# Attention of a hybrid encoder: value products straight behind the scores, transposes over three banks

## The chip, the cores and the metric

The kernel runs on one core of a Trainium2 chip. A core has TensorE (PE in the profile; PEld is its loading of weights), VectorE (DVE), ScalarE (ACT), GpSimd (POOL) and SyncE, whose queue (SPq) issues the transfers here. All data are float32. The metric is the time of one execution on the device in microseconds.

## The reference

Two layers act on two sequences, of 512 and 2048 tokens, 1024 wide. Each layer makes one input projection, then three branches (a recurrence in both directions, attention, a gating branch), and one output projection. The change touches attention alone:

```python
s = einsum('bqhd,bkhd->bhqk', q, k) * 96 ** -0.5     # 6 heads, q and k 96 wide (64 + 32 rotary)
p = softmax(s, axis=-1)
o = einsum('bhqk,bkhd->bqhd', p, v)                  # v 64 wide
```

Each sequence attends to itself, all keys for every query.

## The kernel before, in words

`build` runs the stages of a layer one after the other; each ends with a barrier of all engines. `mla_attention` (L1582) is the fourth of five stages. It reads queries and keys, already transposed (`qkt`, 96 rows per head), and values (`va`) from memory in HBM, and writes `ob`.

Work goes in **slots**, 17 for each of 6 heads, 102 in all (`slots`). Slot 0 of a head is the whole short sequence: four tiles of 128 queries against 512 keys. Each other slot is one tile of 128 queries of the long sequence against its 2048 keys. Either way the scores are 128 x 2048 numbers in banks 0 to 3 of the eight PSUM banks (512 columns of float32 each). Four slots of the long sequence (`TPG`) make a **group**, and so does a head's slot 0: five groups a head.

What happens to slot n:

- `scores(n)` on TensorE: products of 64 rows (two at a time side by side in the array, L1746) and of 32 rows (four side by side, L1751), added in the bank. A bank may be written when the exponentials of slot n-1 have read it (`freed`).
- `maxima(n)` on VectorE: maximum of each row, in two halves (L1875), times -scale (L1877). For a head's slot 0 it is one step over four banks (L1869).
- `exponentials(n, half)` on ScalarE: exp of 1024 columns (L1830), or four of 512 in a head's slot 0 (L1827), into `pr[:, n % 2]`. `exp_count` says how many must be done for each part.
- `turn(n, x)` on TensorE for the parts x = 0 to 3 of 512 columns: four transposes of 128 x 128 into one bank (L1770), 4 for even parts and 5 for odd ones. It waits until the part before in the same bank has been copied.
- `turned_out(n, x)`: the copy of that bank to `PT` in SBUF, parts 0 and 2 by ScalarE (L1839), parts 1 and 3 by VectorE (L1884). ScalarE copies part 0 before its exponentials of the next slot and part 2 behind them.
- `weigh(g, i)` on TensorE: the value products of group g, a pair of key blocks at a time, each of 64 output rows, two side by side (L1786), into bank 6. The list `due` gives each iteration up to two pairs of a group whose last slot lies at least two iterations back. There are 107 iterations; 0, 1, 3, 4 and 5 have no pair, all others have two. From slot 102 on there are only value products.
- When a group is complete (`summed_in`), ScalarE copies bank 6 to `oT` (L1857), TensorE turns it back in iteration n+1 (`turn_out`, four transposes, L1796, into bank 7), and VectorE divides by the sums (`normalise`, L1889 to L1900).

TensorE's order in iteration n is written out: scores of n; part 0 of slot n-1; `turn_out`; part 1; the value products; parts 2 and 3. VectorE's is maxima of n, copy of part 1, `normalise`, copy of part 3.

Each engine executes its own instructions in order; waits are on semaphores that another engine counts up. `act_t` and `dve_t` count the copies, `scored`, `exps`, `turned`, `summed`, `o_out`, `o_turned` and `normed` the other steps.

Transfers are all issued by SyncE in order. At the start of the stage come two for slot 0 of head 0 (`first`), then six for the queries of its other slots (columns 512 to 2560; 64 rows twice, 32 rows four times, as each tile of the array needs its own copy), six for the keys, one for the values, and then head 1. Slot 1 of head 0 waits for the twelve (`arrived[0]`).

Of the kernel before, what the change touches and what calls it, by code (L numbers as in the profile page):

```python
# [27 lines left out]
P = 128  # L28
# [3 lines left out]
T = T0 + T1  # L32
# [1549 lines left out]
def mla_attention(l, late, late_in, nc, d, ps, kc, col, amod, eps, ident):  # L1582
# [6 lines left out]
    KB1 = T1 // P  # L1589
    slots = [(h, s) for h in range(HB) for s in range(NSLOT)]  # L1590
    NS = len(slots)
    BANK_T, BANK_O, BANK_F = 4, 6, 7
    HALF = (slice(0, DN), slice(DN, P))
    STRIP = [slice(DR * n, DR * (n + 1)) for n in range(4)]
    KEYS = (0, 2, 1, 3)
# [23 lines left out]

    def summed_in(n):  # L1620
        return [g for g, i in due[n] if final_pair((g, i))] if 0 <= n < len(due) else []

    def buffer_user_before(g):

# [6 lines left out]
    with ExitStack() as ctx:  # L1631
# [28 lines left out]

        bank = lambda b: ps[:, b, :].rearrange("p (j c) -> p j c", c=P)

        with stage(nc, "in0 in1 first_in v_in0 v_in1 scored maxed exps turned act_t dve_t summed o_out o_turned normed sent0 sent1 zeroed chain") as (
                block, in0, in1, first_in, v_in0, v_in1, scored, maxed, exps, turned, act_t, dve_t, summed, o_out, o_turned, normed, sent0, sent1, zeroed, chain):
            arrived, v_in, sent = (in0, in1), (v_in0, v_in1), (sent0, sent1)

            @block.sync
            def _(sp):
# [31 lines left out]

                for n in range(2):
                    sp.dma_start(first[:, n, :], d["qkt"][HB * DQK * n:HB * DQK * n + DQK, 0:T0]).then_inc(first_in, 16)
                load_queries(0, T0, T, arrived[0])
                load_keys(0, arrived[0])
                load_v(0)
                load_head(1, arrived[1])
                load_v(1)
# [19 lines left out]
            def _(pe):  # L1727
                def scores(n):
                    h, s = slots[n]
                    w = heads_in[h % 2]  # L1730
                    if h == 0 and s == 0:
                        pe.wait_ge(first_in, 32)
                        for c in range(4):
                            pe.matmul(ps[:, c, :], first[:, 0, c * P:(c + 1) * P], first[:, 1, :], start=True, stop=True).then_inc(scored, 1)
                        return
                    if s == (1 if h == 0 else 0):
                        pe.wait_ge(arrived[h % 2], 16 * 18 * (h // 2 + 1) - (16 * 6 if h % 2 == 0 else 0))

                    def freed(c):
                        if n:  # L1740
                            pe.wait_ge(exps, exp_count[n - 1][c])

                    def rows64(c):
                        t, k0 = (c, 0) if s == 0 else (TPG - 1 + s, T0 + G * (KEYS[c] % 2))
                        q, k = w[HALF[c % 2], Q_N + t * P:Q_N + (t + 1) * P], w[HALF[c % 2], K_N + k0:K_N + k0 + G]
                        return pe.matmul(ps[:, c, :], q, k, start=(c < 2), stop=(c >= 2))  # L1746

                    def rows32(c):
                        t, k0 = (c, 0) if s == 0 else (TPG - 1 + s, T0)
                        r = STRIP[KEYS[c]]  # L1750
                        return pe.matmul(ps[:, c, :], w[r, Q_R + t * P:Q_R + (t + 1) * P], w[r, K_R + k0:K_R + k0 + G], start=(c >= 2), stop=(c < 2))  # L1751

                    for c in range(2):
                        freed(c)
                        rows64(c)
                    for c in range(4):
                        if c >= 2:
                            freed(c)
                        last = rows32(c)
                        if c < 2:  # L1760
                            last.then_inc(scored, 1)
                    for c in range(2, 4):
                        rows64(c).then_inc(scored, 1)

                def turn(n, x):
                    pe.wait_ge(exps, exp_count[n][x])
                    if 2 * n + x // 2:
                        pe.wait_ge(dve_t if x % 2 else act_t, 2 * n + x // 2)
                    for k in range(TPG):
                        last = pe.transpose(ps[:, BANK_T + x % 2, k * P:(k + 1) * P],  # L1770
                                            pr[:, n % 2, (TPG * x + k) * P:(TPG * x + k + 1) * P], ident)
                    last.then_inc(turned, 1)

# [16 lines left out]

                def turn_out(g):
                    pe.wait_ge(o_out, g + 1)
                    if g:
                        pe.wait_ge(normed, g)
                    for j in range(TPG):
                        last = pe.transpose(ps[:, BANK_F, j * P:(j + 1) * P], oT[:, g % 2, j * P:(j + 1) * P], ident)  # L1796
                    last.then_inc(o_turned, 1)

                for n in range(len(due) + 1):
                    now = due[n] if n < len(due) else []  # L1800
                    if n < NS:
                        scores(n)
                    turns = 1 <= n <= NS
                    if turns:
                        turn(n - 1, 0)
                    for g in summed_in(n - 1):
                        turn_out(g)
                    if turns:
                        turn(n - 1, 1)
                    for u in now:  # L1810
                        weigh(*u)
                    if turns:
                        turn(n - 1, 2)
                        turn(n - 1, 3)

            @block.scalar
            def _(a):
# [16 lines left out]
                def turned_out(n, x):  # L1834
# [1 line left out]
                    if before is not None:  # L1836
                        a.wait_ge(summed, before + 1)
                    a.wait_ge(turned, 4 * n + x + 1)
                    a.activation(evict_target(n, x), bank(BANK_T), ACT.Copy).then_inc(act_t, 1)  # L1839

                for n in range(len(due)):
                    turns = 1 <= n <= NS
                    if n == 0:
                        a.wait_ge(zeroed, 2)
                    if turns:
                        turned_out(n - 1, 0)
                    if n < NS:
                        exponentials(n, 0)
                    if n < NS:
                        exponentials(n, 1)  # L1850
                    if turns:
                        turned_out(n - 1, 2)
                    for g in summed_in(n):
                        a.wait_ge(summed, g + 1)
                        if g >= 2:
# [4 lines left out]
            def _(v):  # L1860
# [18 lines left out]
                def turned_out(n, x):  # L1879
# [1 line left out]
                    if before is not None:  # L1881
                        v.wait_ge(summed, before + 1)
                    v.wait_ge(turned, 4 * n + x + 1)
                    v.tensor_copy(evict_target(n, x), bank(BANK_T + 1)).then_inc(dve_t, 1)  # L1884

                def normalise(g):
                    h, k = divmod(g, GROUPS)
# [2 lines left out]
                    ch.wait()  # L1890
                    ch.link(v.reciprocal(rec[:, 1, :], rec[:, 0, :]))
                    v.wait_ge(o_turned, g + 1)
                    b = ps[:, BANK_F, :].rearrange("p (j c) -> p j c", c=P)
                    ch.link(v.tensor_copy(halves[:, :, :], b[:, :, 0:DV]))
                    ch.wait()
                    ch.link(v.tensor_tensor(halves[:, :, :], b[:, :, DV:P], halves[:, :, :], ALU.add))
# [4 lines left out]
                                    rec[:, 1, :].unsqueeze(2).to_broadcast([P, TPG, DV]), ALU.mult).then_inc(normed, 1)  # L1901

                for n in range(len(due) + 1):
                    turns = 1 <= n <= NS
                    if n < NS:
                        maxima(n)
                    if turns:
                        turned_out(n - 1, 1)
                    for g in summed_in(n - 1):
                        normalise(g)  # L1910
                    if turns:
                        turned_out(n - 1, 3)


def out_projection(l, late, late_in, cols, sg, nc, d, ps, kc, col, amod, eps, ident):
# [359 lines left out]
```

## Time and profile before

| | us |
|---|---|
| timed, median of 3 runs | 5414.87 (5413.25 to 5425.9) |
| the profiled execution | 5432.9 |
| its span, first to last instruction | 5430.8 |
| TensorE busy in the span | 5145.1 (95%) |
| VectorE busy | 2809.7 (52%) |
| ScalarE busy | 2067.7 (38%) |
| transposes of the attention stages, L1770 | 456.4 |
| value products, L1786 | 370.7 |
| scores, L1746 and L1751 | 231.7 + 230.2 + 117.9 + 117.1 |

Of this span slots 1 to 101 of the first layer take 1622.95 to 2353.96 us, and those of the second begin at 4344.02.

How to read the rows below. A line of the timeline has the start, the length, the engine, the line of the kernel, the operation, what it writes and reads, how many instructions stand in it one behind the other, and in brackets how long the engine had been idle before and who ended that. A matmul's printed length includes its way through the array, so neighbouring lines overlap by about 0.1 us: the distance from one start to the next is what a block really costs. Instructions side by side in the array are counted singly (one float32 product of the scores stands as two instructions). The second view gives for each stretch its length, the busy time of each engine with its number of instructions, the granted clock of TensorE as a share of 2.4 GHz, the busy share of the DMA engines and GB/s.

### The profile page before, as it was taken

The page shows a single profiled execution, that of the slowest core. Times are in us where ns is not written, and L with a number is a line of the kernel's source. Part 1 is how long each engine was busy: PE and PEld are TensorE (multiplying, and loading weights), DVE is VectorE, ACT ScalarE, POOL GpSimd, SP SyncE. Part 2 cuts the span into 40 slices and gives each one's busy share as a digit, 9 for nine tenths or more (in the row PEclk, how much of TensorE's full clock was granted, in tenths as well). Part 3 has the DMA queues.
Part 4 walks back from the last instruction along what each step waited for, and adds up shares of the span by engine and source line. Part 5 has one row for each costly group of instructions (what it writes and reads, how often), then busy time and mean ns, then how long its engine had stood idle before and what let it go on. Part 6 is the DMA issues. An engine that isn't in the chain of part 4 may idle for free. (4 is left out here: it accounts for less than half of the span.)

```text
span 5430.8 us, 98183 instructions
## 1 busy us (share of the span) xinstructions
PE 5145.1 (95%) x40460; PEld 2723.0 (50%) x40460; DVE 2809.7 (52%) x4438; ACT 2067.7 (38%) x3470; POOL 642.5 (12%) x1110
## 2 busy tenths in 40 slices
PE   8999999999979999989989999998899799999899
PEld 3444344478864444434434444444778644444454
DVE  2222387655545565556522214875555455555565
ACT  1121456345545454421112115562455444454211
POOL 0000000044430000001100000000444300000011
PEclk9999999999989999989999999999999899999999
DMA  5311565466551222135343115655555411221353
GB/s 225 141 68 57 185 216 195 156 164 164 146 126 30 46 60 52 37 134 214 111 163 141 68 56 195 217 198 155 151 156 148 117 39 40 57 60 37 108 177 116
DMA packets 579384, 668.56 MB, mean 123 GB/s; under 512 B 231216, under 2 KB 458032, under 8 KB 568384
## 3 DMA queue, kind: packets, MB, share of 16 engines
q1 hardware_dynamic: 578352, 661.17, 39.6%
q8 instruction: 326, 5.34, 0.4%
q14 instruction: 114, 0.93, 0.1%
q10 hardware_dynamic: 592, 1.11, 0.1%
HBM read 395.02 MB, written 267.13 MB: 122 GB/s over the span
## 5 line engine op out<-in xcount | busy, mean ns | idle before, releaser
L490 PE MATMUL ps<-feat_hT,w_features 128*128 128x512 f32 x2240 | 974.2, 593 | 0.0
L810 PE MATMUL ps<-w_tokens,prep_hT 128*128 128x512 f32 (+1 forms) x1920 | 821.7, 588 | 22.0 <-DMA prep_hT<-s_ht 22.0
L490 PEld LDWEIGHTS ps<-feat_hT,w_features 128*128 128x128 f32 x2240 | 421.0, 190 | 507.1 <-issue 504.0
L1875 DVE TENSOR_REDUCE att_mx<-ps 128x1 f32<-128x1024 f32 x384 | 453.5, 1220 | 287.7 <-PE ps L1751 285.3
L810 PEld LDWEIGHTS ps<-w_tokens,prep_hT 128*128 128x128 f32 x1920 | 363.5, 191 | 468.8 <-issue 441.4
L2156 PE MATMUL ps<-w_out,fin_yT 128*128 128x512 f32 x1280 | 569.0, 598 | 2.5 <-DVE fin_yT L2106 2.5
L1770 PEld LDWEIGHTS ps<-kc,att_pr 128*128 128x128 f32 x3264 | 350.8, 140 | 323.4 <-issue 275.6
L1839 ACT ACTIVATE att_PT<-ps 128x512 f32<-128x512 f32 x384 | 229.2, 597 | 631.2 <-PE ps L1770 628.0
L1770 PE MATMUL ps<-kc,att_pr 128*128 128x128 f32 x3264 | 456.4, 280 | 6.0 <-ACT att_PT L1839 2.7
L1830 ACT ACTIVATE att_pr<-ps,att_nb 128x1024 f32<-128x1024 f32 x384 | 424.8, 1111 | 68.7 <-DVE att_nb L1877 68.7
L1884 DVE COPY att_PT<-ps 128x512 f32<-128x512 f32 x384 | 264.1, 688 | 284.5 <-PE ps L1770 283.7
L2156 PEld LDWEIGHTS ps<-w_out,fin_yT 128*128 128x128 f32 x1280 | 238.9, 192 | 274.9 <-issue 271.6
L1786 PE MATMUL ps<-att_PT,att_V 128*64 128x512 f32 x1536 | 370.7, 604 | 0.0
L380 ACT ACTIVATE feat_z<-ps 128x512 f32<-128x512 f32 x110 | 65.7, 597 | 606.1 <-PE ps L490 606.1
L2034 POOL TENSOR_SCALAR fin_rv<-fin_st 128x1 f32<-128x1 f32 x40 | 17.7, 443 | 1970.7 <-DVE fin_st L2052 1970.7
L1746 PE MATMUL ps<-w_out 64*128 64x512 f32 x800 | 230.2, 650 | 15.3 <-DMA w_out<-s_qkt 15.3
L1746 PE MATMUL ps<-att_qk 64*128 64x512 f32 x816 | 231.7, 641 | 0.0
L419 DVE SCALAR_TENSOR_TENSOR feat_co<-feat_z,col,feat_co 128x512 f32<-128x512 f32 (+1 forms) x88 | 66.1, 751 | 297.8 <-ACT feat_co L352 297.8
L404 DVE TENSOR_SCALAR feat_hT<-ps,amod 128x512 f32<-128x512 f32 x80 | 63.7, 809 | 285.2 <-PE ps L477 285.0
L1421 DVE TENSOR_TENSOR scan_tok<-ps,scan_u 64x384 f32<-64x384 f32 x160 | 88.8, 555 | 220.5 <-PE ps L1542 181.1
L1252 POOL TENSOR_SCALAR scan_ss<-scan_ss 128x2 f32<-128x2 f32 x40 | 17.4, 434 | 1443.4 <-ACT scan_csq L1295 1443.4
L704 ACT ACTIVATE prep_st<-ps 128x512 f32<-128x512 f32 (+1 forms) x120 | 68.9, 581 | 269.3 <-PE ps L810 269.3
(234 smaller groups left out, 7204.9 us busy)
## 6 DMA issues: line engine op xcount, KB each, us to landing
s_sc<-prep_sc SPq DMA_DIRECT2D x20, 3072.0 KB, 9.0
scan_src<-s_sc SPq DMA_DIRECT2D x160, 384.0 KB, 4.8
s_qkt<-scan_qT SPq DMA_DIRECT2D x40, 576.0 KB, 4.1
fin_z<-s_zt SPq DMA_DIRECT2D x40, 576.0 KB, 5.1
s_zf<-feat_co SPq DMA_DIRECT2D x88, 256.0 KB, 2.5
s_ht<-feat_hT SPq DMA_DIRECT2D x10, 2048.0 KB, 7.9
prep_hT<-s_ht SPq DMA_DIRECT2D x40, 512.0 KB, 5.7
s_zt<-prep_st SPq DMA_DIRECT2D x80, 256.0 KB, 3.3
```

The source lines that it names most:

```text
L490: last = pe.matmul(b, wf[:, k, i * P:(i + 1) * P], hT[g % 2][:, k, :], start=(k == 0), stop=(k == KD - 1))
L704: a.activation(st[:, n % NB, 0:c1 - c0], ps[:, tiles.bank(pieces[n]), 0:c1 - c0], ACT.Copy).then_inc(z_out, 1)
L810: last = pe.matmul(ps[:, tiles.bank(pieces[n]), 0:c1 - c0], hT[j % NH][:, k, :], wt[:, k, c0:c1], start=(k == 0), stop=(k == KD - 1))
L1421: last = v.tensor_tensor(out_, pair(u, BA * CH)[HALF[p], :, :].rearrange("p o (m i) -> p o m i", m=BA), u0[HALF[p], s, :, :].rearrange("p ...
L1746: return pe.matmul(ps[:, c, :], q, k, start=(c < 2), stop=(c >= 2))
L1770: last = pe.transpose(ps[:, BANK_T + x % 2, k * P:(k + 1) * P], pr[:, n % 2, (TPG * x + k) * P:(TPG * x + k + 1) * P], ident)
L1786: last = pe.matmul(ps[DV * half:DV * half + DV, BANK_O, :], V[:, TPG + TPG * KEYS[kb // TPG] + kb % TPG if k else kb, 0:DV], PT[:, kb, :], ...
L1830: a.activation(pr[:, n % 2, 2 * half * G:2 * (half + 1) * G], ps[:, 2 * half:2 * half + 2, :].rearrange("p b n -> p (b n)"), ACT.Exp, bias ...
L1839: a.activation(evict_target(n, x), bank(BANK_T), ACT.Copy).then_inc(act_t, 1)
L1875: ch.link(v.tensor_reduce(mx[:, n % 2, half:half + 1], ps[:, 2 * half:2 * half + 2, :].rearrange("p b n -> p (b n)"), AX.X, ALU.max))
L1884: v.tensor_copy(evict_target(n, x), bank(BANK_T + 1)).then_inc(dve_t, 1)
L2156: last = pe.matmul(b, yT[n % TPG][:, k, :], wo[:, k, G * c:G * (c + 1)], start=(k == 0), stop=(k == KD - 1))
```

## The change

In the loop over iterations TensorE now does the scores, then the value products, then the four parts one behind the other, then `turn_out`. Parts and turned sums share three banks, 4, 5 and 7, taken in turn in the order in which they occur (`turns`, `place`, `ring`). Each waits for whoever used its bank three places before (`ring_before`, `ring_free`): a part for its copy, a turned sum for its `normalise`.

VectorE now copies the even parts, both ahead of `normalise`, and ScalarE the odd ones: part 1 between the two halves of the exponentials, part 3 behind them.

The queries of head 0 come in two loads: columns 512 to 1024 with the keys on a semaphore of their own (`second_in`, awaited by slot 1), the rest, six transfers more, behind the keys (awaited by slot 5). There is one semaphore more in the stage.

```diff
@@ -1589,7 +1589,7 @@
     KB1 = T1 // P
     slots = [(h, s) for h in range(HB) for s in range(NSLOT)]
     NS = len(slots)
-    BANK_T, BANK_O, BANK_F = 4, 6, 7
+    BANK_O, RING = 6, (4, 5, 7)
     HALF = (slice(0, DN), slice(DN, P))
     STRIP = [slice(DR * n, DR * (n + 1)) for n in range(4)]
     KEYS = (0, 2, 1, 3)
@@ -1619,6 +1619,22 @@
 
     def summed_in(n):
         return [g for g, i in due[n] if final_pair((g, i))] if 0 <= n < len(due) else []
+
+    turns = []
+    for n in range(1, len(due) + 1):
+        if n <= NS:
+            turns += [("x", n - 1, x) for x in range(4)]
+        turns += [("out", g) for g in summed_in(n - 1)]
+    place = {u: i for i, u in enumerate(turns)}
+
+    def ring(*u):
+
+        return RING[place[u] % len(RING)]
+
+    def ring_before(*u):
+
+        i = place[u] - len(RING)
+        return turns[i] if i >= 0 else None
 
     def buffer_user_before(g):
 
@@ -1660,8 +1676,8 @@
 
         bank = lambda b: ps[:, b, :].rearrange("p (j c) -> p j c", c=P)
 
-        with stage(nc, "in0 in1 first_in v_in0 v_in1 scored maxed exps turned act_t dve_t summed o_out o_turned normed sent0 sent1 zeroed chain") as (
-                block, in0, in1, first_in, v_in0, v_in1, scored, maxed, exps, turned, act_t, dve_t, summed, o_out, o_turned, normed, sent0, sent1, zeroed, chain):
+        with stage(nc, "in0 in1 first_in second_in v_in0 v_in1 scored maxed exps turned act_t dve_t summed o_out o_turned normed sent0 sent1 zeroed chain") as (
+                block, in0, in1, first_in, second_in, v_in0, v_in1, scored, maxed, exps, turned, act_t, dve_t, summed, o_out, o_turned, normed, sent0, sent1, zeroed, chain):
             arrived, v_in, sent = (in0, in1), (v_in0, v_in1), (sent0, sent1)
 
             @block.sync
@@ -1700,8 +1716,9 @@
 
                 for n in range(2):
                     sp.dma_start(first[:, n, :], d["qkt"][HB * DQK * n:HB * DQK * n + DQK, 0:T0]).then_inc(first_in, 16)
-                load_queries(0, T0, T, arrived[0])
-                load_keys(0, arrived[0])
+                load_queries(0, T0, T0 + G, second_in)
+                load_keys(0, second_in)
+                load_queries(0, T0 + G, T, arrived[0])
                 load_v(0)
                 load_head(1, arrived[1])
                 load_v(1)
@@ -1733,8 +1750,10 @@
                         for c in range(4):
                             pe.matmul(ps[:, c, :], first[:, 0, c * P:(c + 1) * P], first[:, 1, :], start=True, stop=True).then_inc(scored, 1)
                         return
-                    if s == (1 if h == 0 else 0):
-                        pe.wait_ge(arrived[h % 2], 16 * 18 * (h // 2 + 1) - (16 * 6 if h % 2 == 0 else 0))
+                    if h == 0 and s == 1:
+                        pe.wait_ge(second_in, 16 * 12)
+                    if s == (1 + TPG if h == 0 else 0):
+                        pe.wait_ge(arrived[h % 2], 16 * 18 * (h // 2 + 1) - (16 * 12 if h % 2 == 0 else 0))
 
                     def freed(c):
                         if n:
@@ -1762,12 +1781,22 @@
                     for c in range(2, 4):
                         rows64(c).then_inc(scored, 1)
 
+                def ring_free(*u):
+
+                    before = ring_before(*u)
+                    if before is None:
+                        return
+                    if before[0] == "out":
+                        pe.wait_ge(normed, before[1] + 1)
+                    else:
+                        n, x = before[1:]
+                        pe.wait_ge(act_t if x % 2 else dve_t, 2 * n + x // 2 + 1)
+
                 def turn(n, x):
                     pe.wait_ge(exps, exp_count[n][x])
-                    if 2 * n + x // 2:
-                        pe.wait_ge(dve_t if x % 2 else act_t, 2 * n + x // 2)
+                    ring_free("x", n, x)
                     for k in range(TPG):
-                        last = pe.transpose(ps[:, BANK_T + x % 2, k * P:(k + 1) * P],
+                        last = pe.transpose(ps[:, ring("x", n, x), k * P:(k + 1) * P],
                                             pr[:, n % 2, (TPG * x + k) * P:(TPG * x + k + 1) * P], ident)
                     last.then_inc(turned, 1)
 
@@ -1790,28 +1819,22 @@
 
                 def turn_out(g):
                     pe.wait_ge(o_out, g + 1)
-                    if g:
-                        pe.wait_ge(normed, g)
+                    ring_free("out", g)
                     for j in range(TPG):
-                        last = pe.transpose(ps[:, BANK_F, j * P:(j + 1) * P], oT[:, g % 2, j * P:(j + 1) * P], ident)
+                        last = pe.transpose(ps[:, ring("out", g), j * P:(j + 1) * P], oT[:, g % 2, j * P:(j + 1) * P], ident)
                     last.then_inc(o_turned, 1)
 
                 for n in range(len(due) + 1):
                     now = due[n] if n < len(due) else []
                     if n < NS:
                         scores(n)
-                    turns = 1 <= n <= NS
-                    if turns:
-                        turn(n - 1, 0)
+                    for u in now:
+                        weigh(*u)
+                    if 1 <= n <= NS:
+                        for x in range(4):
+                            turn(n - 1, x)
                     for g in summed_in(n - 1):
                         turn_out(g)
-                    if turns:
-                        turn(n - 1, 1)
-                    for u in now:
-                        weigh(*u)
-                    if turns:
-                        turn(n - 1, 2)
-                        turn(n - 1, 3)
 
             @block.scalar
             def _(a):
@@ -1836,20 +1859,20 @@
                     if before is not None:
                         a.wait_ge(summed, before + 1)
                     a.wait_ge(turned, 4 * n + x + 1)
-                    a.activation(evict_target(n, x), bank(BANK_T), ACT.Copy).then_inc(act_t, 1)
+                    a.activation(evict_target(n, x), bank(ring("x", n, x)), ACT.Copy).then_inc(act_t, 1)
 
                 for n in range(len(due)):
-                    turns = 1 <= n <= NS
+                    turning = 1 <= n <= NS
                     if n == 0:
                         a.wait_ge(zeroed, 2)
-                    if turns:
-                        turned_out(n - 1, 0)
                     if n < NS:
                         exponentials(n, 0)
+                    if turning:
+                        turned_out(n - 1, 1)
                     if n < NS:
                         exponentials(n, 1)
-                    if turns:
-                        turned_out(n - 1, 2)
+                    if turning:
+                        turned_out(n - 1, 3)
                     for g in summed_in(n):
                         a.wait_ge(summed, g + 1)
                         if g >= 2:
@@ -1881,7 +1904,7 @@
                     if before is not None:
                         v.wait_ge(summed, before + 1)
                     v.wait_ge(turned, 4 * n + x + 1)
-                    v.tensor_copy(evict_target(n, x), bank(BANK_T + 1)).then_inc(dve_t, 1)
+                    v.tensor_copy(evict_target(n, x), bank(ring("x", n, x))).then_inc(dve_t, 1)
 
                 def normalise(g):
                     h, k = divmod(g, GROUPS)
@@ -1890,7 +1913,7 @@
                     ch.wait()
                     ch.link(v.reciprocal(rec[:, 1, :], rec[:, 0, :]))
                     v.wait_ge(o_turned, g + 1)
-                    b = ps[:, BANK_F, :].rearrange("p (j c) -> p j c", c=P)
+                    b = bank(ring("out", g))
                     ch.link(v.tensor_copy(halves[:, :, :], b[:, :, 0:DV]))
                     ch.wait()
                     ch.link(v.tensor_tensor(halves[:, :, :], b[:, :, DV:P], halves[:, :, :], ALU.add))
@@ -1901,15 +1924,14 @@
                                     rec[:, 1, :].unsqueeze(2).to_broadcast([P, TPG, DV]), ALU.mult).then_inc(normed, 1)
 
                 for n in range(len(due) + 1):
-                    turns = 1 <= n <= NS
+                    turning = 1 <= n <= NS
                     if n < NS:
                         maxima(n)
-                    if turns:
-                        turned_out(n - 1, 1)
+                    if turning:
+                        turned_out(n - 1, 0)
+                        turned_out(n - 1, 2)
                     for g in summed_in(n - 1):
                         normalise(g)
-                    if turns:
-                        turned_out(n - 1, 3)
 
 
 def out_projection(l, late, late_in, cols, sg, nc, d, ps, kc, col, amod, eps, ident):
```

## Rows read from the trace of the kernel before

**Rows 1.** Slots 1 to 101, layer 0: us, PE, PEld, DVE, ACT, POOL busy, clock
```profile
1622.95:2353.96 731.01, 728.64 (x4120) 327.65 (x4120) 430.26 (x639) 360.53 (x654) 0.00 (x0) 1.00 0.19 44
```

**Rows 2.** TensorE by time, a slot: start, length, group [idle before <-releaser]
```profile
1801.30 1.09 PE L1770 MATMUL ps<-kc,att_pr 128*128 128x128 f32 x8
1802.33 1.13 PE L1746 MATMUL ps<-att_qk 64*128 64x512 f32 x4
1803.38 1.14 PE L1751 MATMUL ps<-att_qk 32*128 32x512 f32 x8
...
1805.52 1.09 PE L1770 MATMUL ps<-kc,att_pr 128*128 128x128 f32 x8
1806.54 1.94 PE L1786 MATMUL ps<-att_PT,att_V 128*64 128x512 f32 x8
1808.41 1.09 PE L1770 MATMUL ps<-kc,att_pr 128*128 128x128 f32 x8
1809.43 1.13 PE L1746 MATMUL ps<-att_qk 64*128 64x512 f32 x4
```

**Rows 3.** VectorE in order of time, same slot
```profile
1802.50 0.69 DVE L1884 COPY att_PT<-ps 128x512 f32<-128x512 f32 x1 [1.82 <-PE ps L1770]
...
1806.98 0.21 DVE L1877 TENSOR_SCALAR att_nb<-att_mx 128x1 f32<-128x1 f32 x1
```

**Rows 4.** ScalarE in order of time, same slot
```profile
1807.23 1.11 ACT L1830 ACTIVATE att_pr<-ps,att_nb 128x1024 f32<-128x1024 f32 x1 [0.36 <-DVE att_nb L1877]
...
1809.42 0.59 ACT L1839 ACTIVATE att_PT<-ps 128x512 f32<-128x512 f32 x1
1809.90 0.60 ACT L1857 ACTIVATE att_oT<-ps 128x512 f32<-128x512 f32 x1
```

**Rows 5.** TensorE in order of time: other runs of transposes
```profile
1112.20 1.97 PE L1484 MATMUL ps<-kc,scan_src 128*128 128x128 f32 x16
...
1812.62 0.66 PE L1770 MATMUL ps<-kc,att_pr 128*128 128x128 f32 x4
1813.11 0.60 PE L1796 MATMUL ps<-kc,att_oT 128*128 128x128 f32 x4
1813.55 0.60 PE L1770 MATMUL ps<-kc,att_pr 128*128 128x128 f32 x4
```

**Rows 6.** All engines in order of time: slots without value products
```profile
1645.19 1.13 PE L1746 MATMUL ps<-w_out 64*128 64x512 f32 x4
...
1649.97 0.68 DVE L1884 COPY att_PT<-ps 128x512 f32<-128x512 f32 x1
...
1650.80 0.63 PE L1770 MATMUL ps<-kc,att_pr 128*128 128x128 f32 x4 [0.34 <-DVE att_PT L1884]
...
1651.36 1.13 PE L1746 MATMUL ps<-w_out 64*128 64x512 f32 x4
```

**Rows 7.** All engines in order of time: the slot after a head's first
```profile
1743.69 1.35 PE L1746 MATMUL ps<-att_qk 64*128 64x512 f32 x4
...
1744.42 0.69 ACT L1827 ACTIVATE att_pr<-ps,att_nb 128x512 f32<-128x512 f32 x1
...
1746.31 1.13 PE L1746 MATMUL ps<-att_qk 64*128 64x512 f32 x4
```

**Rows 8.** All engines in order of time: start of each attention stage
```profile
1612.46 0.43 SPq L1699 DMA_DIRECT2D att_V<-s_va  x1
...
1620.04 0.68 ACT L1827 ACTIVATE att_pr<-ps,att_nb 128x512 f32<-128x512 f32 x1
...
1622.95 2.08 PE L1746 MATMUL ps<-w_out 64*128 64x512 f32 x4 [7.50 <-DMA w_out<-s_qkt]
...
4344.02 2.08 PE L1746 MATMUL ps<-w_out 64*128 64x512 f32 x4 [7.82 <-DMA w_out<-s_qkt]
```

**Rows 9.** Line L477 alone by stretches: us, busy (x), clock, DMA, GB/s
```profile
2742.31:2745.07 2.76, 2.76 (x13) 2.76 (x14) 0.50 1.05 393
2745.08:2747.30 2.22, 2.22 (x21) 2.03 (x19) 1.00 1.06 392
```

## The prediction

> **What bounds the kernel now.** I read the busy time of the two attention stages first. Over the first one's 101 slot periods TensorE is busy for 728.64 of 731.01 us, at a granted clock of 1.00 [rows 1]; I take the second layer's stage as alike, since it runs the same code. Nothing else matters unless it makes TensorE wait. Then I read TensorE's instructions of one slot in order of time [rows 2]. A block lasts from its first start to the next block's first start (the printed lengths run past it, as ends overlap): scores 1802.33 to 1805.52, 3.19 us; transposes of parts 0 and 1, 1.02; value products 1.87; transposes of parts 2 and 3, 1.02. Together 7.10, with no idle time in brackets. Slots in which a group's sums are turned as well take four transposes more, 0.44 (1813.11 to 1813.55) [rows 5]. VectorE and ScalarE wait for TensorE in every slot [rows 3, 4]: they have room, so what counts is at what instant they answer it.
>
> **Why a block costs more than its stream.** Four transposes print 0.66, eight 1.09 [rows 2, 5]: 0.11 each. A run of eight at that pace alone would be 0.87, but it takes 1.02: about 0.15 is the price of entering and leaving a run. A run of 16 elsewhere in this kernel prints 1.97 [rows 5], and by the same overlap (1.09 against 1.02) hands over after 1.90. Two runs of eight take 2.04. So with everything ready, one run of 16 saves 0.14 to 0.16 a slot, if scores to value products costs as much as scores to transposes did.
>
> **But the fourth part needs the first one's bank.** Before, banks 4 and 5 alternate, yet the value products stand between parts 1 and 2, which gives the copies 1.87 us. After, the order of banks is 4, 5, 7, 4: part 3 always (with or without a turned group between slots) needs the bank that part 0 had. VectorE must have emptied it, and only parts 1 and 2, eight transposes or 0.87 us, lie between. I work the chain out from the start t of the run:
> part 0's last transpose ends at t+0.66 [rows 5]. VectorE starts its copy 0.11 after such an end (1801.30+1.09 is 1802.39, the copy starts 1802.50) and takes 0.69 [rows 2, 3]: done t+1.46. TensorE restarts 0.15 after the copy (1649.97+0.68 against 1650.80) [rows 6]: part 3 starts at t+1.60 to 1.61, where its turn is t+0.49+0.44+0.44, 1.37 (the first four hand over to more transposes after 0.49, the next after 0.44) [rows 5]. From restart to the next scores four transposes take 0.56 (1650.80 to 1651.36) [rows 6]. The run takes 2.16 in place of 1.90. VectorE is free in time: its slot's last small step ends at 1807.19, 4.86 after the scores began [rows 3], while part 0 is ready at 3.19+1.87+0.66, 5.72. Thus 2.16 against 2.04: **plus 0.11 a slot** (the rows' second decimal allows 0.10 to 0.13), not minus 0.15. A slot with transposes, value products and scores occurs 97 times a layer (slot 2, and 6 to 101), 194 in all: 194 x 0.11 = **+21.3 us**. Bounds: fully hidden it is 194 x -0.15 = -29; with a dearer entry into the value products, below, +40.
>
> **ScalarE's new order.** It copied part 0 before the exponentials and part 2 after them; now it copies part 1 between the two halves. In a full slot: part 1 ends at t+1.09, the copy starts 0.10 later, the second exponential 0.48 after that (1809.42 to 1809.90) [rows 4], and TensorE answers 1.27 after an exponential begins (exponentials begin 4.90 after the scores: 1807.23 less 1802.33, so 1650.09 in the slot of 1645.19, whose next scores start at 1651.36) [rows 2, 4, 6]: t+2.94. The scores' second half wants it at t+2.16+1.05, 3.21 [rows 2]: hidden, by 0.27. It is not hidden in two places.
> - Slots without value products (1, 3, 4, 5 of a layer), period 6.17 now [rows 6]. Exponentials begin 4.90 after the scores, two start 1.10 apart (2.19 for both) [rows 4]; with the copy in between, the second half's scores are released at 4.90+1.10+0.48+1.27 = 7.75, against 6.18+1.06 = 7.24. So 0.5 more each, eight times: **+4.0** (0 to 5).
> - At a new head, four exponentials of 512 columns release the scores one by one; TensorE's last block there starts at 1746.31, 1.06 after a release 0.83 behind the start of the last one, 1744.42 [rows 7]. TensorE waits there already. A copy (0.48) before the third delays this to 1746.79. Of that 0.11 is in the 194 above: 0.37 x 10 = **+3.7** (0 to 5).
>
> **First queries in two parts.** Slot 1 starts at 1622.95 after 7.50 idle on DMA, 7.82 in the second layer [rows 8]. By the code's shapes the twelve transfers before it carry 2.75 MB and would carry 1.25; the next issue after them starts at 1612.46 [rows 8], and would still, as they stay twelve. At 0.5 us an issue the twelve begin at about 1606, and 2.75 MB took the 17 us to 1622.95; 1.5 MB less at that pace is 9 us less: landed at about 1614. Then another wait takes over: slot 0's second exponential starts only at 1620.04 on ScalarE [rows 8], and releases the second bank 0.83 later, as above, 1620.87. So of 7.50 only 2.1 comes back, and 2.4 in the second layer. This stretch runs at half clock (its first score block prints 2.08, a later one 1.13) [rows 2, 8]; an earlier start may bring the rise earlier. **-4.8** (-4 to -8). The other six transfers are wanted by slot 5, over 20 us later; six more issues of 0.5 us leave the bytes ahead of head 0's values as they are, and slot 2 asks for those only at its value products. No price. The end of a stage has the same waits in another order (a turn of sums now lies among the last value products): 0 (-1 to +1).
>
> **Sum.** 21.3 + 4.0 + 3.7 - 4.8 = +24.2 us. The profiled execution took 5432.9 (span 5430.8), so its like would take 5457; the timed runs' median was 5414.87, 18 lower, and gives **5439**.
>
> **A rule against the entry price.** Entering and leaving a run of transposes costs 0.15 here, and the runs after scores and after value products last the same 1.02 [rows 2]. The Trainium skill, TensorEngine Tiling (Array Packing), Overview, says that a change of tiling mode drains the engine. Scores run in row tiles, value products in column tiles, transposes in the whole array, so each of these changes is one already and the trace agrees with a fixed price. The edge scores to value products stands in no row. From the rows' bounds, nothing for it (both kinds of tile flow on) is 194 x -0.15 on the forecast, double is +0.10 x 194.
>
> **Rivals.**
> A. The ring holds: the copy of part 0 is quick enough, the run takes 1.90. For it: three banks in place of two, VectorE idle. Against it: the chain above, every term a row. The point is whether part 0's copy and the two reactions fit into the 0.71 us from the part's end (0.66) to part 3's turn (1.37); they take 0.11+0.69+0.15, 0.95. Then 5439 - 194 x 0.26 = **5389**, faster. Chance 0.12.
> B. The new edge is free: 5439 - 29 = **5410**. Chance 0.10.
> C. The new edge is dear: 5439 + 19 = **5458**. Chance 0.08.
> D. The longer run of transposes lowers the clock. In the other direction the rows speak: a row of transposes that began at 2742.31 went 13 in 2.76 us at a clock of 0.50 and on at once 21 in 2.22 us at 1.00, with nothing else on TensorE: the clock rose among transposes [rows 9]. If they all ran at half clock, 16 x 0.106 more a slot, +330: **5768**. Chance 0.02. The Trainium skill, TensorE: Matmul & The Clock Gate, Part 4, states that transposes don't count as busy for the clock gate; by that this rival would win, and here the trace disagrees.
> The forecast, 5428 to 5452, has 0.62; what I haven't thought of, on either side, 0.06.
>
> **How the numbers follow.** This kernel's runs can tell about 0.3%, 16 us, from no change. Faster than 5399: A and a little, 0.13. Between 5399 and 5431: B, and the low edge of the forecast, 0.21. Slower: 0.66. The range leaves out most of A below and D above: 5396 to 5460.
>
> **What would show it.** In a plain slot of the new kernel: 12 transposes, a gap of about 0.35 to the end printed before it, released by VectorE's copy, 4 transposes, period 7.21 (A: no gap and 6.95; B: gap and 7.06). The first score block after slot 0 at 1620 to 1621 instead of 1623, its idle time ended by ScalarE, no longer by DMA. Slots after a head's first 0.5 longer than now; slots 3 to 5 6.67 instead of 6.17. I am wrong if the gap before part 3 isn't there, or if a score block that hands over to value products lasts much less or more than 3.19.

## The result, and the profile after

The changed kernel takes 5449.32 us (median of 6 runs, 5438.55 to 5456.54) against 5417.42 for the kernel before (6 runs): ratio 1.0056, 95% interval 1.0043 to 1.0069. It is slower by 0.6%; the forecast was 5439. The profiled executions' spans are 5454.6 and 5430.8, 23.8 apart, where the sum had 24.2; that this is so close is partly chance, as the last part of the account below shows.

A plain slot of the first layer, TensorE in order of time; columns as in [rows 2], to which these rows answer:

```profile
1688.15 1.13 PE L1765 MATMUL ps<-w_out 64*128 64x512 f32 x4
1689.21 1.14 PE L1770 MATMUL ps<-w_out 32*128 32x512 f32 x8
1690.28 1.13 PE L1765 MATMUL ps<-w_out 64*128 64x512 f32 x4
1691.34 1.94 PE L1815 MATMUL ps<-att_PT,att_V 128*64 128x512 f32 x8
1693.21 2.23 PE L1799 MATMUL ps<-kc,att_pr 128*128 128x128 f32 x16
1695.37 1.13 PE L1765 MATMUL ps<-w_out 64*128 64x512 f32 x4
```

Scores to value products 3.19, value products 1.87, 16 transposes 2.16: the period is 7.22 where it was 7.10. Scores hand over to value products exactly as they did to transposes, so the edge that no row showed has the ordinary price. The run prints 2.23, and the 16 transposes of [rows 5] print 1.97: the wait sits inside the run, before part 3. The same view, asked from 1694.74 on, begins with part 3:

```profile
1694.81 0.63 PE L1799 MATMUL ps<-kc,att_pr 128*128 128x128 f32 x4
```

That is 1.60 behind the run's start, as forecast, where its turn was 1.37 behind it. No idle time is printed: the printed end of part 2 reaches 0.16 beyond the usual next start, and the view leaves out gaps as small as the 0.07 that remain.

VectorE in the same slot (compare [rows 3]):

```profile
1692.80 0.21 DVE L1900 TENSOR_SCALAR att_nb<-att_mx 128x1 f32<-128x1 f32 x1
1693.97 0.69 DVE L1907 COPY att_PT<-ps 128x512 f32<-128x512 f32 x1 [0.95 <-PE ps L1799]
1694.84 0.69 DVE L1907 COPY att_PT<-ps 128x512 f32<-128x512 f32 x1 [0.18 <-PE ps L1799]
```

It was idle for 0.95 before part 0 was ready, copied it from 1693.97 to 1694.66, and TensorE resumed 0.15 later. The engine that TensorE waits for is 52% busy.

ScalarE in the same slot (compare [rows 4]):

```profile
1693.05 1.12 ACT L1853 ACTIVATE att_pr<-ps,att_nb 128x1024 f32<-128x1024 f32 x1 [4.13 <-DVE att_nb L1900]
...
1694.40 0.60 ACT L1862 ACTIVATE att_PT<-ps 128x512 f32<-128x512 f32 x1
1694.89 1.11 ACT L1853 ACTIVATE att_pr<-ps,att_nb 128x1024 f32<-128x1024 f32 x1
```

The second exponential starts at 1694.89, 0.49 behind the copy's start; 1.27 later, 1696.16, the scores' second half is free, and it is wanted at 1696.43: hidden.

The start of the stage, TensorE by time, and then the same start by stretches (columns as in [rows 1]):

```profile
1614.16 2.65 PE L1765 MATMUL ps<-w_out 64*128 64x512 f32 x4 [4.83 <-ACT att_pr L1850]
1616.74 2.09 PE L1770 MATMUL ps<-w_out 32*128 32x512 f32 x8
1618.76 2.08 PE L1765 MATMUL ps<-w_out 64*128 64x512 f32 x4
1620.77 2.99 PE L1799 MATMUL ps<-kc,att_pr 128*128 128x128 f32 x16
```

```profile
1616.74:1620.77 4.03, 4.03 (x13) 1.02 (x13) 1.23 (x1) 0.00 (x0) 0.00 (x0) 0.50 1.17 233
1620.77:1622.56 1.79, 1.79 (x11) 1.79 (x10) 1.61 (x3) 0.14 (x1) 0.00 (x0) 0.50 1.07 235
1622.57:1623.69 1.12, 1.12 (x9) 0.77 (x8) 0.92 (x2) 1.12 (x3) 0.00 (x0) 1.00 0.92 192
```

The idle time before slot 1 is now ended by ScalarE, as forecast. But the clock rises at about 1622.57, 23.7 after the stage's first issue at 1598.89, and in the kernel before 23.8 after it: in this stage slot 1 starts earlier and the full clock doesn't. Other stages differ, see the item on the first load below.

Slot periods (us), from score start to score start:

| | before | after | forecast |
|---|---|---|---|
| stage's first issue to slot 1, two layers | 17.78, 18.44 | 15.28, 14.85 | about 2.2 less |
| slot 1 | 8.95, 8.63 | 9.53, 9.53 | 0.5 more |
| slots 2 and 6 | 7.12 each | 7.65 each | 0.11 more |
| slots 3, 4, 5 | 6.17 each | 7.30, 6.25, 6.52 | 6.67 each |
| plain full slot | 7.10 | 7.22 | 7.21 |
| with a turned sum | 7.54 | 7.65 | 7.65 |
| slot behind a head's first | 8.03 | 8.54 | 8.5 |
| slots 7 to 100 together, each layer | 682.22 | 695.08 | 694.4 |
| slot 101 to the next stage's first load | 29.26 | 29.96 | the same |
| whole attention stage | 770.95, 771.28 | 785.21, 784.78 | +12.1 each |

### The profile page after: what moved, and what is told of

Read it like the earlier page. It is cut to its first block and busy times, and to the rows that moved or that the text cites. A ratio compares the mean times of both kernels' runs of the same rounds, so it can differ in the third digit from the quotient of the medians.

```text
span 5454.6 us, 98199 instructions
## 1 busy us (share of the span) xinstructions
PE 5166.0 (95%) x40460; PEld 2732.6 (50%) x40460; DVE 2829.6 (52%) x4438; ACT 2058.1 (38%) x3470; POOL 641.3 (12%) x1110
## 5 line engine op out<-in xcount | busy, mean ns | idle before, releaser
L1799 PE MATMUL ps<-kc,att_pr 128*128 128x128 f32 x3264 | 441.1, 278 | 20.5 <-DVE att_PT L1907 6.5
L1815 PEld LDWEIGHTS ps<-att_PT,att_V 128*64 128x64 f32 x1536 | 93.9, 136 | 253.4 <-issue 250.4
```

Of the source, the lines that this page charges most:

```text
L1799: last = pe.transpose(ps[:, ring("x", n, x), k * P:(k + 1) * P], pr[:, n % 2, (TPG * x + k) * P:(TPG * x + k + 1) * P], ident)
L1815: last = pe.matmul(ps[DV * half:DV * half + DV, BANK_O, :], V[:, TPG + TPG * KEYS[kb // TPG] + kb % TPG if k else kb, 0:DV], PT[:, kb, :], ...
```

## The experiments

Theory A is the forecast's: TensorE waits in each slot until VectorE has emptied part 0's bank. Rival B: the new order itself, its edges, the three banks or ScalarE's order, costs the time.

**The copy, the wait and the order, each changed alone.** Each of these four was executed once, with its profile; what they show is read from the periods. First the copy made longer:

```diff
+                    if x == 0:
+                        ch.link(v.tensor_copy(evict_target(n, x), bank(ring("x", n, x))))
+                        ch.wait()
                     v.tensor_copy(evict_target(n, x), bank(ring("x", n, x))).then_inc(dve_t, 1)
```

> The changed kernel, with VectorE's copy of part 0 made twice in every slot (same data, second write on top of the first). Theory A, TensorE waits before part 3 for VectorE's copy of part 0: each full slot becomes longer by what the second copy adds, 0.60 to 0.70 us, so the period 7.22 becomes 7.82 to 7.92 and the profiled execution is 115 to 140 us longer than the changed kernel's 5457. Rival B, the new order of blocks itself costs the time (dearer entries, ScalarE's order): VectorE has 0.9 us of idle time before this copy and more behind it, so the period stays 7.22 and the time stays within 5 us.

5579.83 us, span 5578.0, 123 above the changed kernel's. TensorE, one slot:

```profile
1811.27 1.53 PE L1799 MATMUL ps<-kc,att_pr 128*128 128x128 f32 x12
1813.60 0.63 PE L1799 MATMUL ps<-kc,att_pr 128*128 128x128 f32 x4 [0.80 <-DVE att_PT L1910]
1814.16 0.70 PE L1765 MATMUL ps<-att_qk 64*128 64x512 f32 x2
```

Three parts run, then a gap of 0.80 that VectorE ends; the period is 7.94, plus 0.72, and the second copy began 0.73 behind the first. VectorE has the room, and TensorE still pays for all of it. B is out as the main cause. (Behind a head's first the slots stay at 8.55: there something else ends last.) Next the copy made shorter, the zeroing at the stage's start left out here:

```diff
...
+                    if x == 0:
+                        v.tensor_copy(evict_target(n, x)[:, 0:2, :], bank(ring("x", n, x))[:, 0:2, :]).then_inc(dve_t, 1)
+                        return
                     v.tensor_copy(evict_target(n, x), bank(ring("x", n, x))).then_inc(dve_t, 1)
```

> The changed kernel, with VectorE copying only the first 256 of the 512 columns of part 0; the other half of that part is left out of the computation, and its place in SBUF is zeroed once at the start of the stage. Theory A: the copy takes about 0.40 in place of 0.69, part 3 may start at t+1.32, before its turn at t+1.37, so the gap goes and the period falls from 7.22 to 6.95 or 6.98; 194 slots make -50 us against the changed kernel, a profiled execution of about 5405, 25 below the one of before. Rival B: no change of the period beyond 0.02, profiled execution near 5457.

5404.76 us, span 5403.0, 52 below the changed kernel's. TensorE again:

```profile
1799.10 1.94 PE L1815 MATMUL ps<-att_PT,att_V 128*64 128x512 f32 x8
1800.97 1.97 PE L1799 MATMUL ps<-kc,att_pr 128*128 128x128 f32 x16
1802.86 1.13 PE L1765 MATMUL ps<-att_qk 64*128 64x512 f32 x4
```

The run now takes 1.89 and prints 1.97, as [rows 5] had it for an unhindered one, and the period is 6.95. So the order that was tried is worth 0.15 a slot, once the bank is free in time. Slots with a turned sum took 7.55, 0.16 more than 6.95+0.44. They meet the next occupied bank: the turned sum's turn is three places behind part 1, which ScalarE copies:

```profile
1809.11 0.60 ACT L1862 ACTIVATE att_PT<-ps 128x512 f32<-128x512 f32 x1
```

It ends at 1809.71, and the turned sum starts at 1809.85.

Then the copies' wait for the value products that last read their buffer, kept only in the first slot of a group (the same edit in both engines' `turned_out`):

```diff
...
-                    if before is not None:
+                    if before is not None and x < 2 and (n == 0 or group_of(n - 1) != group_of(n)):
```

> The changed kernel, but the copies wait for the value products that last read their buffer only in the first slot of a group; in the other three slots of a group the order of each engine's own instructions covers it. In the changed trace VectorE starts a copy with one wait 0.04 us after the last transpose has ended, and one with two waits (a semaphore instruction ahead of it) 0.10 to 0.11 after. Theory A: in three of four full slots the period is 7.15 and not 7.22, in the first of a group 7.22; some 145 slots make -10 us. Rival B (the gap comes from something else than the chain through the copy): periods stay 7.22.

5438.87 us, span 5437.1. The one time proves little (the changed kernel's six go down to 5438.55), but the periods do. Of the 67 slots of the first layer's 7 to 100 that have no turned sum and aren't behind a head's first, 62 are at 7.15 and the 5 that open a group at 7.21. Of the 22 with a turned sum, the 17 that open a group stay at 7.65, and the other 5 fall to 7.58. VectorE:

```profile
1803.62 0.69 DVE L1907 COPY att_PT<-ps 128x512 f32<-128x512 f32 x1 [0.89 <-PE ps L1799]
1804.49 0.69 DVE L1907 COPY att_PT<-ps 128x512 f32<-128x512 f32 x1 [0.18 <-PE ps L1799]
```

The run starts at 1802.92, the copy 0.70 behind it; in the changed kernel it is 0.76 (1693.21, 1693.97). A wait that is always met still cost 0.06, since it stood in the chain.

Then the old order of TensorE, all else as changed:

```diff
-                    for u in now:
-                        weigh(*u)
                     if 1 <= n <= NS:
-                        for x in range(4):
-                            turn(n - 1, x)
+                        turn(n - 1, 0)
+                        turn(n - 1, 1)
+                    for u in now:
+                        weigh(*u)
+                    if 1 <= n <= NS:
+                        turn(n - 1, 2)
+                        turn(n - 1, 3)
```

> The changed kernel with one thing back: TensorE again does two parts, the value products, and then two parts. Three banks, the even parts on VectorE, ScalarE's copy of part 1 between the halves of the exponentials, and the split first load stay. Theory A: the value products again stand between part 0 and part 3, so no gap; the period of full slots is 7.10 to 7.11 (7.54 with a turned sum); what is left of the rest is ScalarE's order at a head's start (8.5) and in slots without value products, against a shorter start: the profiled execution is within 6 us of 5433. Rival B, if the three banks or ScalarE's order cost the time: the period stays at 7.2 or more and the time near 5457.

5430.04 us, span 5428.1, beside 5421.02 for the kernel before on the same chip. Plain slots are at 7.10, with a turned sum 7.54, behind a head's first 8.5; slots 3 to 5 take 7.29, 6.25, 6.52. The three banks cost nothing in plain slots, the run of 16 costs the 0.11, and ScalarE's order, which stayed, what the forecast had at heads.

**The parts alone, with repeated executions.** The first queries in two loads on the kernel before (the semaphore and the waits left out here), and the reverse edit, one load again, on the changed kernel:

```diff
...
-                load_queries(0, T0, T, arrived[0])
-                load_keys(0, arrived[0])
+                load_queries(0, T0, T0 + G, second_in)
+                load_keys(0, second_in)
+                load_queries(0, T0 + G, T, arrived[0])
...
```

> The kernel before with one part of the change: the first queries in two loads (slot 1 waits for columns 512 to 1024 and the keys alone). TensorE's order, banks and the roles of VectorE and ScalarE stay. Theory A: slot 1 starts when slot 0's exponentials release it, 2.1 to 3 us earlier in each layer, and all periods from slot 2 on stay 7.10 (8.03 at head starts, 6.17 in slots 3 to 5): -4 to -6 us on the time of before, 5417. Rival B, the later transfers (values of head 0, head 1) come late and give it back: 0.

> The changed kernel with the first queries in one load again. Theory A: periods as in the changed kernel (7.22, 7.65, 8.54), the start of slot 1 as in the kernel before (17.8 to 18.4 us behind the stage's first issue): 4 to 6 us above the changed kernel's 5449. Rival B, the split is worth nothing under the new order: 5449.

Split alone: 5419.83 (11 runs) against 5419.24 (15 runs), ratio 0.9999 (0.9990 to 1.0008). Order alone: 5449.25 (5 runs), ratio 1.0054 (1.0042 to 1.0067), where the changed kernel has 1.0056. So the split is worth nothing that can be measured, and both expectations put 4 to 6 us on it; the interval reaches from 5 us faster to 4 slower, so it makes a gain of that size unlikely and doesn't rule it out. In the profile of the split alone slot 1 starts 2.6 and 3.1 us earlier, slot 1's period is 10.0 and 9.9 for 8.95 and 8.63, and the stage saves 1.0 and 1.2.

Third, the wait kept only in a group's first slot, as above, and ScalarE's order mended (only the second edit is shown):

```diff
...
+                    late_copy = n < NS and (slots[n][1] == 0 or not due[n])
                     if n < NS:
                         exponentials(n, 0)
-                    if turning:
+                    if turning and not late_copy:
                         turned_out(n - 1, 1)
                     if n < NS:
                         exponentials(n, 1)
                     if turning:
+                        if late_copy:
+                            turned_out(n - 1, 1)
                         turned_out(n - 1, 3)
...
```

> The changed kernel with two edits: copies wait for their buffer only in the first slot of a group (as in the run before with that edit: -9 us), and where slot n is a head's first or has no value products, ScalarE copies part 1 behind both halves of the exponentials and not between them. Theory A: head starts fall from 8.5 to about 8.2 and slots 4 and 5 from 6.25 and 6.5 to about 6.2, 2 to 4 us a layer; all other slots are at 7.15 with the gap before part 3 still there. Time 5449 - 9 - 6, 5434, still 0.2 to 0.4% above the kernel before. Rival B, ScalarE's order is what keeps the kernel slower: the time comes to 5417 or less.

5438.47 us (5 runs), ratio 1.0035 (1.0022 to 1.0047), 4 above the expected 5434. Behind a head's first 8.1, slots 4 and 5 at 6.25 and 6.17 in the second layer: the term at heads was ScalarE's copy. Slots 2 and 6 fell from 7.65 to 7.16. But slot 3 takes 8.38, not less: its turned sum has part 1's bank, which ScalarE now empties behind both exponentials. TensorE, slot 3 of the first layer:

```profile
1642.25 0.63 PE L1799 MATMUL ps<-kc,att_pr 128*128 128x128 f32 x4 [0.89 <-DVE att_PT L1910]
1644.47 0.63 PE L1824 MATMUL ps<-kc,att_oT 128*128 128x128 f32 x4 [1.59 <-ACT att_PT L1862]
1645.03 1.59 PE L1765 MATMUL ps<-w_out 64*128 64x512 f32 x4
```

**A version that beats both.** What the runs say together: a change of blocks costs 0.15, and a run over three banks is free up to 12 transposes. So, on the kernel before with three banks in turn, slots are paired. The first of a pair has no run before its value products and 12 transposes behind them; the second begins with part 3 left over and part 0, and has 12 behind. Seven blocks in place of eight, none of 16.

```diff
+        if defers(n):
+            late_outs, outs_now = outs_now, []
+            pre.append([])
+            post.append(xs[0:3])
...
+        elif n and defers(n - 1):
+            pre.append([("x", n - 2, 3), xs[0]])
+            post.append(xs[1:4])
...
+                    for u in pre[n]:
+                        turn_out(u[1]) if u[0] == "out" else turn(*u[1:])
+                    for u in now:
+                        weigh(*u)
+                    for u in post[n]:
+                        turn(*u[1:])
...
```

> The kernel before, with three banks in turn, but never more than three parts in a run. In 45 pairs of slots per layer TensorE does, in the first slot of a pair, scores, value products, parts 0 to 2 of the slot behind (3 blocks), and in the second scores, the part 3 left over and part 0 (and a turned sum), value products, parts 1 to 3 (4 blocks). Engines are assigned so that each bank is free at its turn, and ScalarE copies before or behind both halves of the exponentials, never between. Theory A: a run of up to 12 transposes over three banks meets no occupied bank, so one change of blocks is saved in every pair without a gap: 6.52 and 7.54 in place of 7.10 twice, 0.15 a pair, 90 pairs: -13 us on the kernel before, and at a head's start up to 0.4 less each: 5401 to 5408, faster than both. Rival B (long runs cost what they save, whatever the bank): periods sum to 14.2 or more, time 5417 or above.

5403.35 us (6 runs) against 5418.81 (10 runs): ratio 0.9970, interval 0.9958 to 0.9982. TensorE, a pair, the second slot with a turned sum:

```profile
1802.49 1.13 PE L1800 MATMUL ps<-att_qk 64*128 64x512 f32 x4
...
1805.68 1.94 PE L1849 MATMUL ps<-att_PT,att_V 128*64 128x512 f32 x8
1807.55 1.53 PE L1833 MATMUL ps<-kc,att_pr 128*128 128x128 f32 x12
1809.01 1.13 PE L1800 MATMUL ps<-att_qk 64*128 64x512 f32 x4
...
1812.20 1.09 PE L1833 MATMUL ps<-kc,att_pr 128*128 128x128 f32 x8
1813.13 0.60 PE L1858 MATMUL ps<-kc,att_oT 128*128 128x128 f32 x4
1813.66 1.94 PE L1849 MATMUL ps<-att_PT,att_V 128*64 128x512 f32 x8
1815.53 1.53 PE L1833 MATMUL ps<-kc,att_pr 128*128 128x128 f32 x12
1816.99 1.13 PE L1800 MATMUL ps<-att_qk 64*128 64x512 f32 x4
```

6.52 and 7.98 (7.54 without the sum); slots 7 to 100 take 673.81, 8.4 less than before in each layer. The run of 12 lasts 1.46 (1807.55 to 1809.01), which is 8 transposes' 1.02 and four more at 0.11: no wait inside it.

## Why the prediction was right

- **The gap before part 3** (+21.3). Right in mechanism and size: 7.22 for a forecast 7.21, a run of 2.16 for 2.16; it answered one for one to a longer copy, vanished with a shorter one, and went with the old order. Slots 7 to 100, heads included, came to +12.86 a layer where the terms give +12.2. Four slots of the profiled execution are longer by some 0.36 each, because VectorE began a copy that much late, for a reason that the trace doesn't show; no slot of the kernel before is longer in this way. They make up most of the remaining difference. One sign was wrong: I wanted a printed gap of 0.35, and in a plain slot none is printed. By the forecast's own chain part 3 starts at t+1.60 and the end printed before it is t+1.53, which leaves 0.07.
- **ScalarE's order at heads** (+3.7): 8.54 for 8.5, and 8.1 with the copy behind.
- **Slots without value products** (+4.0): 4.8 by the profile, and the slots weren't those that I named. For slots 3 to 5 the sum 20.07 for three times 6.67, 20.01, is chance: slot 3 was 0.6 longer, as its turned sum waited for part 1's bank, a wait that I missed; slots 4 and 5 were shorter. Slots 2 and 6, each behind a slot without value products, took 7.65, 0.43 above a plain slot: the late release holds up the scores behind. With the old order of TensorE they took 7.60, with ScalarE's mended 7.16, so it is ScalarE's copy. That makes 1.56 and twice 0.43 in each layer.
- **The first load** (-4.8). This term was too large. Slot 1 started earlier as worked out, and the start to slot 2's scores, 26.73 and 27.07 before, became 24.81 and 24.38, 1.9 and 2.7 less. That looks like the forecast's 4.8 and is largely chance, for this profile of the kernel before has the slowest starts on record: with the same single load the order alone took 25.22 and 26.01, the paired version 25.78 and 24.43. Where the load alone differs, both stages together save 2.2 (split alone against before) and 0.9 (changed kernel against order alone), and timed runs nothing measurable. I had counted on full-rate microseconds, and part of what was gained was time at half rate. When the clock rose varied: in the ten profiles' twenty stages it was 20.0 to 23.8 us after the stage's first issue with one load (six stages) and 18.2 to 23.9 with two (fourteen). In the run with the waits reduced, the first layer's stage, it rose 18.6 after the issue at 1600.37, and slot 2 began 22.85 after it:

```profile
1614.74:1618.95 4.21, 4.21 (x12) 1.48 (x12) 0.00 (x0) 1.86 (x6) 0.00 (x0) 0.50 1.24 198
1618.96:1623.22 4.26, 3.36 (x25) 2.01 (x21) 3.76 (x5) 1.27 (x3) 0.00 (x0) 1.00 1.11 232
```

So an earlier start sometimes came with an earlier rise, and in the changed kernel's first stage not; what decides it is open. Besides, slot 1's second bank is released 0.65 after the first, and its first block prints 2.65 for 2.08 [rows 8].

- **The end of the stage** (0): +0.7 a layer. With the order alone it is 0.2, with the split alone 0.5; in that profile clearing the stage's semaphores took 0.5 longer. Whether the one semaphore more does that I haven't tested.
- **The whole.** The two attention stages grew by 27.8 us: 25.7 in slots 7 to 100, 5.2 in slots 2 to 6, 1.4 at the ends, less 4.6 up to slot 2. The rest of the profiled span, the same code, was 4.0 shorter, and in all ten profiles it lies between 3874.6 and 3888.6 us, longest in that of the kernel before. So 23.8 beside 24.2 is luck in part. The timed medians differ by 31.9, inside an interval of 23 to 37. The forecast's 24 lies at its lower end, mainly for the 4.8 of which some 1 to 2 was there. An estimate with the measured pieces, 3.3 for the load, 0.8 for slots without value products, 1.3 for slots 7 to 100 and 0.4 for the ends on top of 24.2, comes to 30.0.

Rivals A (5389), B (5410) and C (5458) fell with the 7.22 and the 3.19; the time alone, 5449, lies between the forecast and C. D fell too: in both attention stages the granted clock stayed 1.00 from its rise, 23.7 and 22.0 us after the first issue, until behind the last block. The edge that stood in no row, scores to value products, has the price of the others. (What the forecast takes from the Trainium skill, TensorEngine Tiling (Array Packing), on a change of tiling mode stands there under Tiling Modes, Key Properties.)

## What to carry to other kernels

Before joining runs on the engine that bounds the kernel, count the buffers in the run: the run is only as long as its banks, and the time from the last write of a bank to its reuse must hold the copy and both reactions (here 0.11 + 0.69 + 0.15 us against 0.71). An engine at half load can be the bound if its answer is awaited at once; idle time elsewhere is no slack in such a chain. Fewer changes of blocks do pay, here 0.15 us each, when the joined runs stay short enough for the banks.

## What the runs showed of the hardware

A second wait on an instruction that sits in such a chain costs about 0.07 us though it is long met (7.22 against 7.15); in the trace it stands as a semaphore instruction ahead of the copy. And in the run with the waits reduced and ScalarE's order mended, TensorE's idle 0.89 and 1.59 us within slot 3 of the first layer was followed by the half clock:

```profile
1639.83:1645.03 5.20, 2.72 (x23) 2.13 (x21) 3.08 (x7) 3.27 (x6) 0.00 (x0) 1.00 1.23 236
1645.60:1648.60 3.00, 3.00 (x14) 0.55 (x10) 0.84 (x2) 0.00 (x0) 0.00 (x0) 0.50 0.06 22
1648.90:1652.00 3.10, 2.44 (x16) 1.44 (x14) 3.03 (x5) 0.54 (x1) 0.00 (x0) 0.99 0.00 0
```

Slot 4 took 7.78 there for 6.25 in the second layer, where the same idle time left the clock alone. The same stall cost nothing more in one stage and another 1.5 us in the other.
